# A two-model fp32 forward pass on one core: the first model's token mixing gets its first VectorE split earlier, its first gated scores on ScalarE, one product in a named PSUM bank, the rotary sines ahead of the splits; at two stage changes one split moves behind the normalisation

## The chip, the core and the metric

One core of one Trainium2 chip runs the whole program as one launch. The metric is the device time of that launch in microseconds (us). Runs of this kernel before the change took 2380.64 us (median of 3, from 2380.03 to 2381.09).

## What is computed

Two transformer models run one after the other, with float32 inputs and outputs. The change touches the first model only (two layers, width 1024, 256 tokens x and 256 context tokens z). Each of its layers is, in short:

```python
x, z = x + 0.5*g*ffn1(...), z + 0.5*g*ffn1(...)     # SwiGLU, hidden width 2816
px, pz = split_in(hx @ w_in), split_in(hz @ w_in)   # 15 kinds of columns
a = fourier_mix(p.fourier)                          # 2-D DFT
b = neighborhood_attention(na_q, na_k, na_v, ctx k and v, bias)
c = gla_output(bidir_gla(q, k, v, gates))           # gated linear attention, chunks
d = block_attention(rope(gqa_q), rope(gqa_k), gqa_v)
x = x + g*(concat(a, b, c, d) @ w_out)              # z as well, in layer 0 only
x = x + 0.5*g*ffn2(...)                             # z as well, in layer 0 only
```

Each sub-block starts with an RMS norm and a per-channel scale and shift (the modulation). The second model (two layers of softmax attention with forget gates beside retention, and a SwiGLU) follows on x and 16 meta tokens.

In the gated attention the score of query i and key j is a sum over 32 channels of q·k·decay. The kernel builds it by levels: a first, undecayed product q·k (times 2) gives the diagonal of each 128x128 tile, and seven masked levels overwrite the rest of it.

## The kernel before

**Weights and splits.** Every big product is done as three single-pass float32r matmuls: high weight times high input, high weight times low input, low weight times high input (lines 815 to 817). The weights stream from HBM in units of 128 x 1024 into a ring of six. For every unit ScalarE writes the high part into one of four `ring_high` buffers (line 1393) and VectorE writes the low part over the ring slot (line 1916), both in functions called `split_ahead`. ScalarE's split of a unit waits until TensorE has finished with the unit four splits earlier. TensorE's `weights()` waits for the low part. `split_ahead(1)` in step k of the mixing handles the unit that TensorE uses in step k + 4.

**The mixing.** A layer's `mixing` runs MIX_STEPS = 21 steps. TensorE, ScalarE and VectorE each have a function `mixing(l)` with the same step counter k; every engine works through its own list in order and the engines are tied by semaphores only. Step k does the projection of item k of PROJ1 (24 matmuls, about 5.8 us with 512 columns, half of it with 256) and, around it, small jobs. On TensorE the order within a step is: the attention scores of the tile whose turn is k + 1, the four products `gla_pairs(l, k - 10)` for 9 <= k <= 17, the projection, `head_mean`, the rope `rotation`, `turn` (transposes of the probabilities, line 1157), `values` (probabilities times V, line 1169). So step 9 does the first, undecayed pairs, number -1, and step 10 the pairs of level 0 (both line 1191). On VectorE step k does: the sines of rope items (`rope_sin`, line 2241), the row maxima of the scores (`maxima`, lines 2283 to 2308), the head norm (`qk_norm`, line 2229), the rope sum, `mixed_low` (line 2336: it reads what `values` left in its bank and so frees the bank), the doubling of the first pairs into `gla_scores` in step 9 (line 2421) or the masked copy of a level in steps 10 to 16 (line 2431), then `project`: the eviction of the projection (line 2211), `normalise` of the probabilities (line 2332), and the split of step k. On ScalarE step k does: `turned` (line 1647), `mixed_high` (line 1656), the squares for the head norm (line 1590), the decays' exponential (line 1713), the softmax exponentials (lines 1615 and 1616), its own evictions (line 1577), the high half of the split (line 1393), then the head norm's root (lines 1400 and 1403).

**PSUM banks.** TensorE has eight banks. `take(key)` gives the next one in rotation and first waits until what was in it, eight takes before, is freed; `take_at(b, key)` gives bank b by name, waits for its last user, and does not move the rotation. `gla_pairs` takes all its four banks before its first matmul.

```python
            def gla_pairs(l, v):
                ...
                ps = [take("pairs", l, v, h) for h in range(4)]
```

The takes around step 9 are, in order, in layer 0: scores (two, banks 7 and 0), pairs -1 (1, 2, 3, 4), projection 9 (5), a head mean (6), `values` of the z pair (7); then in step 10 scores (0, 1), pairs 0 (2, 3, 4, 5). In layer 1: scores (6, 7), pairs -1 (0, 1, 2, 3), projection 9 (4), a head mean (5), `values` (6); then in step 10, which has no scores, pairs 0 (7, 0, 1, 2).

**Stage changes.** When a sub-block's last product ends, its output chunks 0 to 7 (of 128 channels each) are added to the residual, squared, summed, and normalised for the next sub-block, for token group 0 (x) and then 1 (z). `norm(tag, g, chunks)` exists on VectorE (lines 1982 and 1991), ScalarE (lines 1441 and 1444) and GpSimd (line 636): VectorE scales a chunk, ScalarE adds the shift and rounds to the high part, and the low part comes from VectorE for even chunks and from GpSimd for odd ones. TensorE meanwhile begins the next sub-block's first units in `first_units`, chunk by chunk, group 0 and then group 1. `late_chunks` (ScalarE, line 1450 on) and `residual` (VectorE, line 2080 on) hold the order of these with the splits. The change's reordering is reached with group 1 after `out1` of layer 0 and after `ffn2` of layer 0, and leaves the order after `ffn1` as it was.

Of the kernel before, what the change touches and what calls it, by code (L numbers as in the profile page):

```python
# [32 lines left out]
ALU = mybir.AluOpType  # L33
# [3 lines left out]
P = 128  # L37
# [182 lines left out]
def build(nc, A, old=None):  # L220
    ev = Events(*(old or (None, None)))
    ctx = ExitStack()
    with ctx:
# [144 lines left out]
        def cst(at, n=P, rows=P):  # L368
            return const[0:rows, at:at + n]
# [412 lines left out]
        def _(pe):  # L782
# [378 lines left out]
            def values(pr):  # L1161
# [3 lines left out]
                p = take("attended", *pr["id"])  # L1165
# [96 lines left out]
            def mixing(l, prev):  # L1262
# [3 lines left out]
                for k in range(MIX_STEPS):  # L1266
# [19 lines left out]
                    for pr in owed_at(l, k):  # L1286
                        values(pr)
# [89 lines left out]
        def _(act):  # L1377
# [80 lines left out]
            def late_chunks(tag, h):  # L1458
# [19 lines left out]
                norm(tag, 1, range(4))  # L1478
                if tag[0] != "ffn1":
                    split_ahead(1)  # L1480
                norm(tag, 1, range(4, KC))
# [203 lines left out]
            def mixing(l):  # L1685
# [3 lines left out]
                for k in range(MIX_STEPS):  # L1689
# [20 lines left out]
                    if LEVEL_STEP - 1 <= k < LEVEL_STEP + LEVELS:  # L1710
# [67 lines left out]
            def second_mixing(l):  # L1778
                tp = ("b2", l)
                tiles = fox_tiles(l)  # L1780
                for k in range(FOX_STEPS):
# [18 lines left out]
                    if k == SLOT2[FLOG]:  # L1800
                        act.wait_ge(*when("forget_steps", "flog_neg_abs", l))
                        act.activation(negc[0:8, 1, :], negc[0:8, 1, :], ACT.Exp).then_inc(*made("flog_exp", l))
                        act.wait_ge(*when("flog_exp", l))
                        act.activation(negc[0:8, 1, :], negc[0:8, 1, :], ACT.Ln, bias=eps_one[0:8, 1:2]).then_inc(
                            *made("flog_ln", l))
# [4 lines left out]
                    if k == SLOT2[FLOG] + 1:  # L1810
                        act.wait_ge(*when("forget_steps", "negc", l))
                        act.wait_ge(*when("neg_cleared", l))
                        for e in range(2):
                            r = HD * e
                            act.activation(neg_parts[r:r + 8], negc[0:8, 2, :], ACT.Copy).then_inc(
                                *made("neg_high", l, e))
# [88 lines left out]
        def _(dve):  # L1905
# [175 lines left out]
            def residual(tag, l, m, streams, h, nb, last_part, dots_of=None):  # L2081
# [80 lines left out]
            def project(tag, plan, i, n, src, vtemp, tile=None, between=None, heads=(), items=()):  # L2162
                kind, dst, width = plan[i][:3]
                if i and plan[i - 1][0] == "V" and tag[0] == "mix1" and (i - 1) % 2 == 0:
# [10 lines left out]
                if not on_act(tag, i):  # L2175
# [21 lines left out]
                    elif kind == "T" and FOUR <= dst < FOUR + 2:  # L2197
# [3 lines left out]
                        dve.tensor_copy(x[:, :, P:SEQ], y[:, :, P:SEQ]).then_inc(*made("fold_steps", "upper", tag[1], dst - FOUR))  # L2201
                        dve.wait_ge(*when("fold_steps", "upper", tag[1], dst - FOUR))
                        dve.tensor_tensor(x[:, :, 1:P], y[:, :, 1:P], x[:, :, SEQ - 1:P:-1], ALU.add).then_inc(
                            *made("fold_steps", "even", tag[1], dst - FOUR))
                        dve.wait_ge(*when("fold_steps", "even", tag[1], dst - FOUR))
# [17 lines left out]
                if dst != FLOG:  # L2223
                    split_ahead(1)
# [167 lines left out]
            def mixing(l):  # L2392
# [4 lines left out]
                for k in range(MIX_STEPS):  # L2397
                    for i in means_at(l, k - 2):
                        if i >= 4:
                            rope_sin(tm, i - 4, cst(C_SIN1, NX), NX)  # L2400
# [16 lines left out]
                    if k == LEVEL_STEP:  # L2417
                        for h in range(4):
# [395 lines left out]
```

## Time and profile before

| | |
|---|---|
| runs before | 2380.64 us median (2380.03 to 2381.09) |
| the profiled execution's own time | 2380.5 us |
| its span, first to last instruction | 2378.7 us |
| TensorE matmuls busy | 2353.7 us (99%) |
| VectorE busy | 1533.4 us (64%) |
| ScalarE busy | 1014.2 us (43%) |
| GpSimd busy | 406.8 us (17%) |
| granted TensorE clock, mean | 0.999 |

PE is TensorE's matmul side and PEld its weight loads, DVE is VectorE, ACT ScalarE, POOL GpSimd. Layer 0's mixing lies at about 393 to 575 us of the span, layer 1's at about 1348 to 1485 us. A matmul's shown end is modelled and overlaps the next one's start, so where TensorE's time is summed the starts are compared. A timeline row gives the start, the time from the first start to the last end, the engine, the line, the operation, the tiles written and read, the shapes, the count of merged instructions, and in brackets the idle time before it with what ended that idle time.

### The profile page before, as it was taken

To read this page: it belongs to the slowest core of one execution; us is meant where nothing else is said; L and a number is where in the kernel's file an instruction comes from. 1 tells how busy PE (TensorE), PEld (TensorE's weight loads), DVE (VectorE), ACT (ScalarE), POOL (GpSimd) and SP (SyncE) were. 2 spreads that over 40 slices of the span, in tenths; PEclk is the share of its full clock that TensorE was granted. 3 is DMA by queue.
4 is the path that set the end of the run, shared out by engine and by line. 5 is a ranking of instruction groups with operands and counts; after the bars stand their busy time and mean duration, and the time that the engine had idled before them with its cause. 6 is when DMAs were issued, how large, how long until landed. Compare 5 with 4: busy or idle time off the path is not lost.

```text
span 2378.7 us, 36504 instructions
## 1 busy us (share of the span) xinstructions
PE 2353.7 (99%) x14394; PEld 2041.4 (86%) x14394; DVE 1533.4 (64%) x2611; ACT 1014.2 (43%) x1694; POOL 406.8 (17%) x427
## 2 busy tenths in 40 slices
PE   8999999999999999999999999999999999999998
PEld 6888889777888888888888877999889999989887
DVE  5888765884698865523323586766677665667874
ACT  5222224644522223422223465554455444456663
POOL 2221211240222131111011121121000220000110
PEclk9999999999999999999999999999999999999999
DMA  9565542112366654222222222555533555434553
GB/s 354 195 212 206 184 159 90 64 54 89 120 215 235 245 207 169 89 97 98 98 98 98 80 92 82 177 186 186 171 114 136 173 173 177 153 117 160 190 190 133
DMA packets 97865, 360.76 MB, mean 152 GB/s; under 512 B 11024, under 2 KB 11792, under 8 KB 96544
## 3 DMA queue, kind: packets, MB, share of 16 engines
q1 hardware_dynamic: 75744, 272.84, 33.2%
q0 software_dynamic: 21952, 85.59, 9.9%
q8 instruction: 115, 1.88, 0.3%
q14 instruction: 54, 0.44, 0.1%
HBM read 357.34 MB, written 1.05 MB: 151 GB/s over the span
## 4 chain that ended last, share of the span: by engine, by line
PE 94%; DVE 2%; ACT 1%; issue 1%; DMA 1%; POOL 0%; DVEq 0%; ACTq 0%; POOLq 0%
PE bank L815 26%; PE bank L817 25%; PE bank L816 25%; PE bank L822 6%; PE bank L823 3%; PE bank L1169 1%; PE bank L1139 1%; PE bank L1157 1%; PE bank L1191 1%; DVE ring_low L1916 1%; DMA arena<-w_mod_first_dram 1%; PE bank L1118 0%; PE bank L1078 0%; ACT ring_high L1393 0%; PE bank L1342 0%
## 5 line engine op out<-in xcount | busy, mean ns | idle before, releaser
L1916 DVE TENSOR_TENSOR ring_low<-ring,ring_high 128x1024 fp32r<-128x1024 f32 x520 | 642.0, 1235 | 484.3 <-ACT ring_high L1393 482.4
L815 PE MATMUL bank<-x_parts,ring_high 128*128 128x512 f32 (+2 forms) x2308 | 799.7, 347 | 4.8 <-POOL x_parts L636 2.2
L1393 ACT ACTIVATE ring_high<-ring 128x1024 fp32r<-128x1024 f32 x520 | 547.9, 1054 | 576.3 <-PE bank L817 532.9
L817 PE MATMUL bank<-x_parts,ring_low 128*128 128x512 f32 (+2 forms) x2308 | 786.2, 341 | 0.0
L816 PE MATMUL bank<-x_parts,ring_high 128*128 128x512 f32 (+2 forms) x2308 | 784.9, 340 | 0.0
L815 PEld LDWEIGHTS bank<-x_parts,ring_high 128*128 128x128 f32 x2308 | 434.5, 188 | 71.1 <-issue 13.3
L817 PEld LDWEIGHTS bank<-x_parts,ring_low 128*128 128x128 f32 x2308 | 434.6, 188 | 47.6
L816 PEld LDWEIGHTS bank<-x_parts,ring_high 128*128 128x128 f32 x2308 | 435.0, 188 | 47.0 <-issue 1.0
L646 POOL TENSOR_TENSOR hidden_parts<-fresh,hidden_parts 128x512 fp32r<-128x512 f32 (+2 forms) x132 | 204.1, 1547 | 1005.0 <-ACT hidden_parts L1527 1005.0
L1929 DVE CUSTOM_DVE_ANT_0 mod_products<-mod_ring,csilu 128x1024 bf16<-128x1024 f32 x224 | 300.5, 1378 | 31.8 <-DMA mod_ring<-w_mod_dram 30.5
L815 PE MATMUL bank<-hidden_parts,ring_high 128*128 128x512 f32 (+2 forms) x814 | 280.9, 345 | 0.7 <-POOL hidden_parts L646 0.7
L817 PE MATMUL bank<-hidden_parts,ring_low 128*128 128x512 f32 (+2 forms) x814 | 280.1, 344 | 0.0
L816 PE MATMUL bank<-hidden_parts,ring_high 128*128 128x512 f32 (+2 forms) x814 | 280.1, 344 | 0.0
L815 PEld LDWEIGHTS bank<-hidden_parts,ring_high 128*128 128x128 f32 x814 | 153.6, 189 | 19.3 <-POOL hidden_parts L646 1.1
L816 PEld LDWEIGHTS bank<-hidden_parts,ring_high 128*128 128x128 f32 x814 | 153.6, 189 | 18.2
L817 PEld LDWEIGHTS bank<-hidden_parts,ring_low 128*128 128x128 f32 x814 | 153.5, 189 | 18.0
L1516 ACT ACTIVATE act_out<-bank 128x512 f32<-128x512 f32 x66 | 39.6, 600 | 263.6 <-PE bank L817 263.6
L822 PE MATMUL bank<-x_parts,ring_high 128*128 128x512 f32 x352 | 123.2, 393 | 0.0
L822 PE MATMUL bank<-hidden_parts,ring_high 128*128 128x512 f32 x308 | 106.9, 392 | 0.0
L815 PE MATMUL bank<-early_parts,ring_high 128*128 128x258 f32 x352 | 99.9, 284 | 0.0
L817 PE MATMUL bank<-early_parts,ring_low 128*128 128x258 f32 x352 | 99.3, 282 | 0.0
L816 PE MATMUL bank<-early_parts,ring_high 128*128 128x258 f32 x352 | 99.3, 282 | 0.0
(267 smaller groups left out, 2757.7 us busy)
## 6 DMA issues: line engine op xcount, KB each, us to landing
ring<-stream_dram SPq DMA_DIRECT2D x517, 512.0 KB, 3.3
mod_ring<-w_mod_dram POOLq DMA_DIRECT2D x128, 512.0 KB, 4.4
arena<-w_mod_first_dram POOLq DMA_DIRECT2D x8, 1024.0 KB, 11.8
ring<-stream_dram POOLq DMA_DIRECT2D x3, 512.0 KB, 10.6
arena<-na_bias_dram POOLq DMA_DIRECT2D x2, 768.0 KB, 12.1
mod_ring<-consts_dram POOLq DMA_DIRECT2D x1, 1076.0 KB, 5.3
resid<-x_dram POOLq DMA_DIRECT2D x2, 512.0 KB, 5.9
resid<-ctx_dram POOLq DMA_DIRECT2D x2, 512.0 KB, 7.1
```

What stands on the lines that cost most here:

```text
L646: pool.tensor_tensor(lo[:, f], fresh[:, f % 2, 0:n], hi[:, f].bitcast(F32), ALU.subtract).then_inc(*made("hidden_low", tag, h, f))
L815: pe.matmul(out, w[0][:, b], xh, start=start, stop=False)
L816: pe.matmul(out, w[0][:, b], xl, start=False, stop=False)
L817: return pe.matmul(out, w[1][:, b], xh, start=False, stop=stop)
L822: pe.matmul(bank.rearrange("p (k n) -> p k n", k=2), w[0][:, b], both, start=start, stop=False)
L823: return pe.matmul(bank[:, 0:NX], w[1][:, b], high, start=False, stop=stop)
L1139: mm = pe.matmul(out, pr["q"][r, q:q + nq], pr["k"][r, 0:NZ if twin else nk], start=not fox, stop=True, skip_group_check=nq < P)
L1157: mm = pe.transpose(p[0:rows, kt * P:kt * P + nq], probs[0:nq, b, e, kt * P:kt * P + rows], cst(C_IDENT, nq, nq))
L1393: act.activation(high[:, i % SPLIT], ring[:, u % LOADED], ACT.Copy).then_inc(high_parts, 1)
L1516: act.activation(act_out[:, f % 2, 0:n], p[:, 0:n], ACT.Silu).then_inc(*made("silu", tag, h, f, frees=("gate", tag, h, f)))
L1916: dve.tensor_tensor(low[:, u % LOADED], ring[:, u % LOADED], high_f[:, i % SPLIT], ALU.subtract).then_inc(low_parts, 1)
L1929: dve.tensor_tensor_reduce(junk[:, s], mod_ring[:, n % MOD_RING], csilu[:, s], 1.0, 0.0, ALU.mult, ALU.add, mod[:, l, s, j:j + 1]).then_in ...
```

## The change

It does six things; the renamed semaphore families (`fold_steps` and `first_sum_steps` become `gate_steps`, `flog_exp`, `flog_ln` and `neg_high` become `forget_act`) are increments and waits of the same instructions under another name.

```diff
 PE:   def values(pr, b=None):
                 pe.wait_ge(*when(*pr["v_ready"]))
                 for j in range(len(pr["tiles"])):
                     pe.wait_ge(*when("probs_t", *pr["id"], j))
-                p = take("attended", *pr["id"])
+                p = take("attended", *pr["id"]) if b is None else take_at(b, "attended", *pr["id"])
...
                     for pr in owed_at(l, k):
-                        values(pr)
+                        values(pr, ev.banks["pairs", l, -1, 0] if k == LEVEL_STEP else None)
...
 ACT:  late_chunks
                 root_of_mean(tag, 1)
-                norm(tag, 1, range(4))
+                norm(tag, 1, range(KC))
                 if tag[0] != "ffn1":
                     split_ahead(1)
-                norm(tag, 1, range(4, KC))
...
 ACT:  mixing, after the decays' exponential, before exps
+                    if k == LEVEL_STEP:
+                        for h in range(4):
+                            act.wait_ge(*when("pairs", l, -1, h))
+                            p = bank("pairs", l, -1, h)
+                            act.activation(gla_s[:, h, 0:n // P], p[:, 0:n].rearrange("p (t n) -> p t n", n=P), ACT.Copy,
+                                           scale=2.0).then_inc(*made("gla_first", l, h, frees=("pairs", l, -1, h)))
...
 DVE:  residual
-                norm(tag, 1, range(4))
+                norm(tag, 1, range(KC))
                 if tag[0] != "ffn1":
                     split_ahead(1)
-                norm(tag, 1, range(4, KC))
...
 DVE:  project
+                if i == 0 and tag[0] == "mix1":
+                    split_ahead(1)
...
                 for item in items:
                     qk_norm(tag[1], item)
-                if dst != FLOG:
+                for item in rotated:
+                    rope_sin(tag, item - 4, cst(C_SIN1, NX), NX)
+                if dst != FLOG and (i or tag[0] != "mix1"):
                     split_ahead(1)
...
 DVE:  mixing
-                    for i in means_at(l, k - 2):
-                        if i >= 4:
-                            rope_sin(tm, i - 4, cst(C_SIN1, NX), NX)
...
-                    if k == LEVEL_STEP:
-                        for h in range(4):
-                            dve.wait_ge(*when("pairs", l, -1, h))
-                            p = bank("pairs", l, -1, h)
-                            dve.tensor_scalar(gla_s[:, h, 0:ntile], p[:, 0:n].rearrange("p (t n) -> p t n", n=P), 2.0,
-                                              None, ALU.mult).then_inc(
-                                                  *made("gla_scores", l, -1, h, frees=("pairs", l, -1, h)))
...
-                            dve.wait_ge(*when("gla_scores", l, v - 1, h))
+                            dve.wait_ge(*(when("gla_scores", l, v - 1, h) if v else when("gla_first", l, h)))
...
                         project(tm, PROJ1, k, width1(l, PROJ1[k]), proj1, VTEMP1, turns.get(k + 1),
-                                items=root_first(l, k))
+                                items=root_first(l, k), rotated=[i for i in means_at(l, k - 1) if i >= 4])
```

In words: (1) `values` of step 9 goes into the bank of the first pairs' head 0 instead of the next in rotation. (2) The doubling of the first pairs goes from VectorE to ScalarE. (3) In step 0 VectorE does its split before it waits for the projection. (4) The rope sines are done at the end of the step before, ahead of that step's split, not after it. (5) and (6) After `out1` and `ffn2` of layer 0 the fourth split comes behind all eight chunks of group 1's norm, on ScalarE and on VectorE.

## Rows read from the trace of the kernel before

**Rows 1.** The page: the chain that ended last, by engine.
```profile
PE 94%; DVE 2%; ACT 1%; issue 1%; DMA 1%; POOL 0%; DVEq 0%; ACTq 0%; POOLq 0%
```

**Rows 2.** Waits of TensorE, 1344 to 1480 us (layer 1's mixing): total, times, longest.
```profile
PE bank L1169 <- ACT arena L1616: 1.6, 1, 1.6
PE bank L815 <- DVE ring_low L1916: 1.6, 1, 1.6
PE bank L1191 <- DVE arena L2211: 1.1, 1, 1.1
```

**Rows 3.** Timeline of the stage change after `out1` of layer 0, several engines.
```profile
629.81 1.23 DVE L1916 TENSOR_TENSOR ring_low<-ring,ring_high 128x1024 fp32r<-128x1024 f32 x1 [1.05 <-ACT ring_high L1393]
...
632.55 0.39 PE L815 MATMUL bank<-x_parts,ring_high 128*128 128x256 f32 x1
...
633.93 0.38 PE L815 MATMUL bank<-x_parts,ring_high 128*128 128x256 f32 x1 [0.40 <-POOL x_parts L636]
...
639.06 0.40 PE L815 MATMUL bank<-x_parts,ring_high 128*128 128x512 f32 x1
```

**Rows 4.** The same after `ffn2` of layer 0.
```profile
994.99 1.23 DVE L1916 TENSOR_TENSOR ring_low<-ring,ring_high 128x1024 fp32r<-128x1024 f32 x1 [1.05 <-ACT ring_high L1393]
...
999.11 0.38 PE L815 MATMUL bank<-x_parts,ring_high 128*128 128x256 f32 x1 [0.40 <-POOL x_parts L636]
```

**Rows 5.** Timeline, layer 1, steps 0 to 4: ScalarE, VectorE, TensorE.
```profile
1362.02 1.04 ACT L1393 ACTIVATE ring_high<-ring 128x1024 fp32r<-128x1024 f32 x1
...
1365.42 1.06 ACT L1393 ACTIVATE ring_high<-ring 128x1024 fp32r<-128x1024 f32 x1 [2.09 <-PE bank L817]
...
1371.26 0.69 ACT L1400 ACTIVATE rstd<-bank,eps_one 128x512 f32<-128x512 f32 x1 [0.32 <-PE bank L1118]
...
1365.42 0.69 DVE L2211 TENSOR_SCALAR arena<-bank 128x512 f32<-128x512 f32 x1 [3.38 <-PE bank L817]
1366.03 2.35 DVE L1916 TENSOR_TENSOR ring_low<-ring,ring_high 128x1024 fp32r<-128x1024 f32 x2
...
1367.30 0.50 PE L815 MATMUL bank<-x_parts,ring_high 128*128 128x512 f32 x1 [1.56 <-DVE ring_low L1916]
```

**Rows 6.** Timeline, layer 1, steps 8 to 10: TensorE.
```profile
1405.54 1.02 PE L1118 MATMUL bank<-squares,const 128*128 128x512 f32 x2
1408.15 1.95 PE L1169 MATMUL bank<-arena 128*64 128x256 f32 x16 [1.58 <-ACT arena L1616]
1410.03 0.73 PE L1191 MATMUL bank<-mod_ring 32*128 32x128 f32 x16
```

**Rows 7.** The same steps: VectorE, then ScalarE.
```profile
1412.11 0.42 DVE L2336 TENSOR_TENSOR mixed_parts<-bank,mixed_parts 128x256 fp32r<-128x256 f32 x1
...
1406.95 0.51 ACT L1615 ACTIVATE arena<-arena,softmax_stats 128x256 f32<-128x256 f32 x1 [3.70 <-DVE softmax_stats L2302]
...
1411.32 0.37 ACT L1656 ACTIVATE mixed_parts<-bank 128x256 fp32r<-128x256 f32 x1
```

**Rows 8.** Timeline, layer 0, steps 9 and 10: TensorE, VectorE, ScalarE.
```profile
465.83 1.17 PE L1191 MATMUL bank<-mod_ring 32*128 32x128 f32 x32
...
468.39 0.41 DVE L2336 TENSOR_TENSOR mixed_parts<-bank,mixed_parts 128x256 fp32r<-128x256 f32 x1
...
463.00 0.60 ACT L1577 ACTIVATE arena<-bank 128x512 f32<-128x512 f32 x1 [2.84 <-PE bank L817]
```

**Rows 9.** Timeline, layer 0, step 11: VectorE, TensorE.
```profile
476.34 0.42 DVE L2241 TENSOR_TENSOR fresh<-bank,const 128x256 f32<-128x256 f32 x1
...
477.01 1.17 PE L1191 MATMUL bank<-mod_ring 32*128 32x128 f32 x32 [0.66 <-DVE fresh L2241]
```

**Rows 10.** Stretches: us, busy of PE, PEld, DVE, ACT, POOL, granted clock, DMA share, GB/s.
```profile
2369.00:2373.80 4.80, 0.94 (x5) 0.34 (x3) 2.63 (x7) 1.31 (x3) 0.00 (x0) 1.00 0.00 0
2373.80:2378.70 4.90, 0.00 (x0) 0.00 (x0) 1.81 (x5) 0.00 (x0) 0.00 (x0) 0.50 0.52 214
1405.70:1408.20 2.50, 0.92 (x5) 0.12 (x4) 2.50 (x12) 1.25 (x5) 1.18 (x4) 1.00 0.51 184
```

More of the change, by code:

```diff
@@ L1159, in turn, with values @@
                     mm.then_inc(*made("turned", *pr["id"], j, e))
-            def values(pr):
+            def values(pr, b=None):
                 pe.wait_ge(*when(*pr["v_ready"]))
@@ L1801, in second_mixing @@
                         act.wait_ge(*when("forget_steps", "flog_neg_abs", l))
-                        act.activation(negc[0:8, 1, :], negc[0:8, 1, :], ACT.Exp).then_inc(*made("flog_exp", l))
-                        act.wait_ge(*when("flog_exp", l))
+                        act.activation(negc[0:8, 1, :], negc[0:8, 1, :], ACT.Exp).then_inc(*made("forget_act", "exp", l))
+                        act.wait_ge(*when("forget_act", "exp", l))
                         act.activation(negc[0:8, 1, :], negc[0:8, 1, :], ACT.Ln, bias=eps_one[0:8, 1:2]).then_inc(
-                            *made("flog_ln", l))
+                            *made("forget_act", "ln", l))
                     if k in tiles:
@@ L2200, in project @@
                         dve.tensor_copy(x[:, :, 0:1], y[:, :, 0:1])
-                        dve.tensor_copy(x[:, :, P:SEQ], y[:, :, P:SEQ]).then_inc(*made("fold_steps", "upper", tag[1], dst - FOUR))
-                        dve.wait_ge(*when("fold_steps", "upper", tag[1], dst - FOUR))
+                        dve.tensor_copy(x[:, :, P:SEQ], y[:, :, P:SEQ]).then_inc(*made("gate_steps", "upper", tag[1], dst - FOUR))
+                        dve.wait_ge(*when("gate_steps", "upper", tag[1], dst - FOUR))
                         dve.tensor_tensor(x[:, :, 1:P], y[:, :, 1:P], x[:, :, SEQ - 1:P:-1], ALU.add).then_inc(
-                            *made("fold_steps", "even", tag[1], dst - FOUR))
-                        dve.wait_ge(*when("fold_steps", "even", tag[1], dst - FOUR))
+                            *made("gate_steps", "even", tag[1], dst - FOUR))
+                        dve.wait_ge(*when("gate_steps", "even", tag[1], dst - FOUR))
                         dve.tensor_tensor(x[:, :, P + 1:SEQ], y[:, :, P - 1:0:-1], x[:, :, P + 1:SEQ],
@@ L2533, in forget_gates @@
                 if k == SLOT2[FLOG] + 1:
-                    dve.wait_ge(*when("flog_ln", l))
+                    dve.wait_ge(*when("forget_act", "ln", l))
                     dve.scalar_tensor_tensor(e, y, 0.0, e, ALU.min, ALU.subtract).then_inc(*made("forget_steps", "flog_log", l))
@@ L2543, in forget_rest @@
                 dve.wait_ge(*when("forget_steps", "negc", l))
-                dve.wait_ge(*when("neg_high", l, 1))
+                dve.wait_ge(*when("forget_act", "neg_high", l, 1))
                 for e in range(2):
@@ L2621, in _ @@
                 dve.tensor_tensor(scaled[:, 0:4, a:b], scaled[:, 0:4, a:b], scaled[:, 4:8, a:b], ALU.add).then_inc(
-                    *made("first_sum_steps", "first_fours", g))
-                dve.wait_ge(*when("first_sum_steps", "first_fours", g))
+                    *made("gate_steps", "first_fours", g))
+                dve.wait_ge(*when("gate_steps", "first_fours", g))
                 dve.tensor_tensor(scaled[:, 0:2, a:b], scaled[:, 0:2, a:b], scaled[:, 2:4, a:b], ALU.add).then_inc(
-                    *made("first_sum_steps", "first_twos", g))
-                dve.wait_ge(*when("first_sum_steps", "first_twos", g))
+                    *made("gate_steps", "first_twos", g))
+                dve.wait_ge(*when("gate_steps", "first_twos", g))
                 dve.tensor_tensor(sumsq[:, a:b], scaled[:, 0, a:b], scaled[:, 1, a:b], ALU.add).then_inc(
```

4 lines of the change are left out of this document (2 added, 2 removed).

## The prediction

> **What bounds the kernel now.** I read the page's busy times and its chain by engine first, then TensorE's waits, then the timelines around each of those waits. TensorE is 94% of the chain [rows 1], and the change removes no matmul. So it can only give or take TensorE's idle gaps, and only those in the first model's two mixings and at two stage changes. In layer 1's mixing the waits come to 1.6, 1.6 and 1.1 us plus smaller ones [rows 2], in layer 0's to one of 0.7 us that matters [rows 9], and each stage change has one near 0.4 us [rows 3, 4]. All of it together is near 6 us of 2380, and 0.2% of the time is 4.8 us, about what a measurement of this kernel can tell from no change. I look at starts, since a matmul's shown end overlaps the next start.
>
> **Fourth split last.** After `out1` of layer 0 VectorE idles 1.05 us for ScalarE's high half and then splits for 1.14 us (629.81 to the next instruction at 630.95) before it normalises chunks 4 to 7 of group 1 [rows 3]. TensorE starts chunk 4 at 632.55 and chunk 5, for which it waited on GpSimd, at 633.93; the six matmuls between take 0.82 when nothing waits (0.12 from start to start, and 0.1 more for the first after a stop), so 0.56 us are lost, and before 632.55 another 0.19 us. With the split behind, the chunks come 1.05 + 1.14 = 2.2 us earlier, more than both losses: minus 0.75 us. The moved split then ends near 634.2 instead of 631.0; TensorE starts that unit at 639.06 now [rows 3], 638.3 then, so the split has 4 us of cover, and without it every us beyond would be paid. After `ffn2` of layer 0 the rows are the same to 0.01 us [rows 4] (0.56 and 0.17 lost): minus 0.73. Sum **minus 1.5 us**. No DMA is issued by the moved steps; ScalarE's table load behind the norm comes 1.1 us sooner.
>
> **Step 0's split first.** In layer 1 TensorE could start step 4 at 1365.58 and starts at 1367.30, when the first low half is written (the merged row at 1366.03 holds the splits of steps 0 and 1) [rows 5]. Its high half was ready at 1363.06, while VectorE idled 3.38 us for the projection. Done then, it ends near 1364.2, and the 1.72 us go. What is late next: VectorE's split of step 1 has to wait for its own high half, 1366.48 [rows 5], so the gate's eviction comes 0.65 to 0.7 us sooner, and ScalarE, which then does the gate's shift, a high half and the roots back to back, starts the first root 1.09 us sooner than 1371.26 (it loses its 0.32 us of idle as well) [rows 5]. From there to step 9 the chain runs through VectorE and ScalarE, not TensorE, so the waits in steps 6 and 9 (0.5 and 1.1 us) keep their place in that chain and TensorE reaches the first pairs **1.09 us earlier**, not 1.72. In layer 0 TensorE has no wait there, so I take nothing.
>
> **First pairs on ScalarE.** VectorE loses four instructions in each layer. ScalarE gains four. No row has this copy on ScalarE; the nearest is its eviction of 128x512 at 0.60 us each [rows 8], so at most 2.4 us in layer 0, and half at 256 columns. It stands before the softmax exponentials, behind which ScalarE idles 2.84 us in layer 0 [rows 8] and in front of which it idles 3.70 us in layer 1 [rows 7]. That is the cover: cost nothing. If it were gone, the exponentials and the evictions queued behind them would be late by up to 2.4 us. The gain on VectorE is nothing either: in layer 1 it waits for those exponentials and then for the next high half.
>
> **Values in the pairs' bank.** Here two waits trade places. Now, in layer 1, `values` takes the bank of the scores in rotation, and waits for the exponentials (L1616) until 1408.15; the means before it began at 1405.54 and need 0.86, so 1.75 us are lost [rows 6]. In the new bank it needs only the first of ScalarE's four copies, long done. That wait goes. But the next four takes are the pairs of level 0, and since the rotation was not moved, they reach the bank that `values` has just filled: in layer 1 they take banks 6, 7, 0, 1 in the old numbering and `values` sits in 0; in layer 0, 1, 2, 3, 4 and `values` sits in 1. All four are taken before the first matmul, so step 10's pairs and the projection behind them wait for `mixed_low` (L2336) of that very pair, on VectorE in step 10.
> - Layer 0: TensorE starts these pairs at 465.83, and L2336 ends at 468.80 [rows 8], because VectorE first does the maxima of scores that TensorE ends just before the pairs, and a head norm. New start 468.84: **plus 3.0 us**.
> - Layer 1: L2336 runs 1412.11 to 1412.53, behind ScalarE's roots and `mixed_high` [rows 7]; 1.09 us earlier that is 1411.44, a start at 1411.48 against 1410.03 now [rows 6]: **plus 1.45 us**, with the 1.09 and the 1.75 already in it. TensorE then stands idle for about 4.2 us in one piece.
>
> Behind both, VectorE and ScalarE have been waiting for TensorE's projection, so the delay passes whole to the end. The later bank waits keep their distance of eight takes.
>
> **The clock in that gap.** The longest stop of TensorE in the steady part is the one before 1408.15, and the granted clock there is 1.00; after the last matmul (1.00 up to 2373.80) it is 0.50, that is 1.2 instead of 2.4 GHz [rows 10]. By these rows a gap of 4.2 us lies between what did not cost the clock and what did. The Trainium skill ("TensorE: Matmul & The Clock Gate", "HAM oscillation — how this bites in real kernels") says that a gap in TensorE's work can bring the slow clock back, so that the next matmuls start cold. By rows 10 alone the sum stays as it is; by that rule the rival below is due.
>
> **Sines ahead of splits.** In layer 0 the pairs of level 1 wait for the bank of the rotation, freed by L2241 after a split of 1.14 us: start 477.01 where 476.28 was possible [rows 9]. With the sine ahead the wait goes: minus 0.7 us. The splits come 0.4 us later and are used four steps on. In layer 1 nothing waits there. The remaining fold wait (0.4 us) is not touched.
>
> **Sum.** Against the profiled execution's own 2380.5 us (its span 2378.7): minus 1.5; layer 0 plus 3.0 minus 0.7; layer 1 plus 1.45. That is plus 2.3, 2382.8 us; the median of the runs is 0.1 above that execution, so **2382.9 us**. Ends of the unknowns: the first layer's pairs between plus 2.5 and plus 3.5; ScalarE's copies 0 to plus 1.2; the 1.09 between 0.5 and 1.72 (1 us either way). With these alone, 2380.8 to 2385.2.
>
> **Rivals.**
> - *The clock falls in the new gap.* Against it: rows 10's third row. For it: the second. Price: no row shows a matmul at 1.2 GHz; a projection of 5.8 us would take twice that, so between 0 and plus 5.8; I take half, plus 2.9: 2385.8 us. It decides if the gap in layer 1 is above 4 us. Chance 0.18.
> - *The bank is free in time* (the other side, faster). If `mixed_low` were through when the pairs ask, before 465.83 in layer 0 and 1407.3 in layer 1, the change would give all it removes: 1.5 + 0.7 + 1.09 + 1.75 = 5.0 us, 2375.6 us. For it: only that VectorE is relieved of L2421. Against it: L2336 waits for scores and roots, not for VectorE's time. Chance 0.12.
> - *Nothing arrives.* The gains are taken back by the VectorE and ScalarE chain, and the new bank wait is half of mine: 2380.6 us. For it: the chain of steps 4 to 9 already eats a third of the first gain. Chance 0.09.
> - The forecast: 0.61.
>
> **Numbers.** Faster than 2375.9: three quarters of the second rival, 0.09. Slower than 2385.4: two thirds of the first and 0.07 of the forecast's tail, 0.19. Within: 0.72. The range takes the forecast's own ends, the clock rival with half of its upper price, and stops short of the fast rival: 2377.0 to 2387.5.
>
> **What would show it.** Right: TensorE's waits list L1191 behind DVE L2336 twice, near 3.0 and 4.2 us; the waits behind ACT L1616, DVE L1916 (1.6 us) and DVE L2241 are gone; the third wait at the stage changes (POOL L636) shrinks by 0.8 us over both. Wrong: if level 0's pairs start without a wait in step 10, the bank step fails and the time is near 2375.6; if the granted clock shows 0.50 anywhere between 1408 and 1425 us, the first rival holds; if step 4 of layer 1 still waits for L1916, the first split is not early.

## The result, and the profile after

| | before | after |
|---|---|---|
| median of 10 runs on the same chip | 2380.44 us (2379.88 to 2381.09) | 2386.78 us (2384.26 to 2388.50) |
| ratio | | 1.0027, 95% interval 1.0019 to 1.0035 |
| the profiled execution's own time | 2380.5 us | 2384.26 us, the fastest of the ten |
| its span | 2378.7 us | 2382.5 us |
| mean granted clock over the ten runs | 0.999 | 0.996 to 0.999 |

The change makes the kernel slower by 6.3 us, 0.27%. Two things are in this table besides the loss: the runs spread over 4.2 us where those of before spread over 1.2, and the profiled execution, whose rows follow, is 2.5 us below the median. So the rows can explain 3.8 us, and 2.5 us need runs.

TensorE's waits over the whole span, the rows that concern the change (line, releaser: us in total, times, longest). The small ones answer to [rows 2] and to the brackets in [rows 3, 4, 9].

```profile
PE bank L1191 <- DVE mixed_parts L2344: 4.3, 1, 4.3
PE bank L1191 <- issue: 2.9, 1, 2.9
...
PE bank L815 <- POOL x_parts L636: 1.4, 4, 0.4
...
PE bank L1191 <- DVE arena L2217: 1.1, 1, 1.1
...
PE bank L1191 <- DVE gla_scores L2429: 0.3, 1, 0.3
PE bank L815 <- POOL hidden_parts L646: 0.2, 1, 0.2
```

Gone are the waits behind the exponentials (1.6 us), behind the first low half (1.6) and behind the sine (0.7); the wait at the two stage changes fell from 2.2 us in all to 1.4. In their place stand 4.3 and 2.9 us ahead of the first level's pairs (L1191).

Layer 0, steps 9 and 10, VectorE and TensorE (answers to [rows 8]):

```profile
467.66 0.74 DVE L2237 SCALAR_TENSOR_TENSOR arena<-arena,small,rstd 128x512 f32<-128x512 f32 x1
468.32 0.42 DVE L2344 TENSOR_TENSOR mixed_parts<-bank,mixed_parts 128x256 fp32r<-128x256 f32 x1
468.83 1.17 PE L1191 MATMUL bank<-mod_ring 32*128 32x128 f32 x32 [2.91 <-issue]
```

"issue" is what the profile writes when it sees no releaser; the pairs start 0.09 us after L2344 ends, and one run below moves that instruction alone.

Layer 1, the same place, with ScalarE (answers to [rows 6, 7]):

```profile
1405.61 1.95 PE L1169 MATMUL bank<-arena 128*64 128x256 f32 x16
...
1410.42 0.36 ACT L1655 ACTIVATE mixed_parts<-bank 128x256 fp32r<-128x256 f32 x1
...
1410.55 0.75 DVE L2237 SCALAR_TENSOR_TENSOR arena<-arena,small,rstd 128x512 f32<-128x512 f32 x1
...
1411.22 0.42 DVE L2344 TENSOR_TENSOR mixed_parts<-bank,mixed_parts 128x256 fp32r<-128x256 f32 x1
...
1411.89 0.73 PE L1191 MATMUL bank<-mod_ring 32*128 32x128 f32 x16 [4.34 <-DVE mixed_parts L2344]
```

`values` (L1169) no longer waits for the exponentials. It is done at 1407.55, and then TensorE stands still for 4.34 us.

Stretches of the same execution (us, busy of PE, PEld, DVE, ACT, POOL, granted clock, DMA share, GB/s):

```profile
470.00:474.30 4.30, 4.30 (x21) 3.56 (x20) 2.59 (x4) 1.54 (x4) 2.96 (x5) 1.00 0.01 4
...
1407.60:1411.80 4.20, 0.00 (x0) 0.00 (x0) 3.56 (x7) 3.98 (x10) 0.11 (x1) 1.00 0.00 1
...
1412.80:1416.20 3.40, 3.40 (x9) 2.65 (x9) 1.30 (x4) 0.00 (x0) 1.64 (x5) 0.50 0.00 0
1416.20:1420.00 3.80, 3.80 (x18) 3.13 (x18) 0.08 (x1) 0.08 (x1) 0.00 (x0) 1.00 0.00 0
```

Here is the term that the forecast left out. The clock held through the gap of layer 1 and for 0.9 us of work after it, then stood at 0.50 for 3.4 us, at 1.2 GHz in place of 2.4, and came back. In those 3.4 us TensorE was busy without a stop and got through 9 matmuls; in the next 3.8 us it did 18. Behind layer 0's gap of 2.9 us the clock held, in this execution.

Starts of the same TensorE instruction in both traces, compared all along the span, give the whole account of this execution. The offset is the start after the change less the start before it. It stays level for long stretches, and a step is the difference between the level behind a place and the level ahead of it:

| place (time in the trace before) | step, us | offset behind it | forecast |
|---|---|---|---|
| pairs of level 0, layer 0 (465.83; offset ahead of it +0.03) | +2.98 | +3.01 | +3.0 |
| pairs of level 1, layer 0 (477.01) | -0.73 | +2.28 | -0.7 |
| rest of layer 0's mixing (480 to 500) | -0.08 | +2.20 | none |
| first sum of squares at the end of `out1` (610.3) | +0.28 | +2.48 | none |
| stage change after `out1` (632.55 to 634.3) | -0.94 | +1.54 | -0.75 |
| hidden parts of layer 0's `ffn` (750.07) | -0.42 | +1.12 | none |
| stage change after `ffn2` (997.73 to 999.5) | -0.92 | +0.20 | -0.73 |
| step 4 of layer 1 (1367.30) | -1.87 | -1.67 | -1.72 |
| steps 6 to 8 (1382.70, 1387.04) | +0.49, +0.29 | -0.89 | together +0.63 |
| `values` of layer 1 (1408.15) | -1.66 | -2.55 | -1.75 |
| pairs of level 0, layer 1 (1410.03) | +4.42 | +1.87 | +4.29 |
| half clock behind it | +1.57 | +3.44 | 0 |
| pairs of level 1, layer 1 (1424.27) | +0.34 | +3.78 | none |
| sum | | last start +3.79 | +2.3 |

### The profile page after: what moved, and what is told of

Read it like the earlier page. It is cut to its first block and busy times, and to the rows that moved or that the text cites. A ratio compares the mean times of both kernels' runs of the same rounds, so it can differ in the third digit from the quotient of the medians.

```text
span 2382.5 us, 36500 instructions
## 1 busy us (share of the span) xinstructions
PE 2355.2 (99%) x14394; PEld 2042.8 (86%) x14394; DVE 1533.1 (64%) x2603; ACT 1016.6 (43%) x1702; POOL 404.6 (17%) x427
## 5 line engine op out<-in xcount | busy, mean ns | idle before, releaser
L646 POOL TENSOR_TENSOR hidden_parts<-fresh,hidden_parts 128x512 fp32r<-128x512 f32 (+2 forms) x132 | 203.3, 1540 | 1005.4 <-ACT hidden_parts L1526 1005.4
```

The lines of the kernel that those rows point to most:

```text
L646: pool.tensor_tensor(lo[:, f], fresh[:, f % 2, 0:n], hi[:, f].bitcast(F32), ALU.subtract).then_inc(*made("hidden_low", tag, h, f))
```

## The experiments

Twelve kernels, each timed in five rounds beside the kernel before on the same chip. The medians of before in the three sets were 2380.68 us (first four kernels), 2380.63 (next four) and 2380.19 (last four); each difference from before below is against its own. Where kernels of different sets are compared with each other, or with the changed kernel (its own before: 2380.44), the medians are taken as they stand, and some 0.4 us of such a difference can be the set. The 95% interval of a ratio reaches about 0.0009, or 2 us, to either side, so that of a single part of the change (kernels 7 to 9) the starts in the trace tell more than the median. A line number moves by a few lines between the kernels.

### 1. Without the named bank

```diff
-                        values(pr, ev.banks["pairs", l, -1, 0] if k == LEVEL_STEP else None)
+                        values(pr)
```

(on the changed kernel)

> The changed kernel with the values taking the next bank of the rotation again; everything else of the change stays. Theory (the named bank is the whole loss: 3.0 us in layer 0, 2.5 us in layer 1, and about 1.7 us of half clock behind layer 1's gap): the other parts are all that is left, 0.9 + 0.6 us at the two stage changes, 0.7 us of the sine wait, 0.9 to 1.1 us at layer 1's steps 4 to 10, so about 2380.4 - 3.2 = 2377.2 us, granted clock 1.00 from end to end of both mixing stages. Rival (the other parts are worth nothing by themselves, or one of them pulls the clock down): 2380 to 2382 us. Rival (the bank is not the cause): 2386.8 us as the changed kernel.

Measured: 2377.74 us (2377.06 to 2378.25), ratio 0.9988 (0.9979 to 0.9997), 2.9 us below the kernel before and 9.0 below the changed one. Layer 1 there, TensorE:

```profile
1404.55 1.95 PE L1169 MATMUL bank<-arena 128*64 128x256 f32 x16 [1.59 <-ACT arena L1615]
1406.42 0.73 PE L1191 MATMUL bank<-mod_ring 32*128 32x128 f32 x16
```

The pair of waits is back as in [rows 6]: 1.59 us behind the exponentials, none ahead of the pairs, and the granted clock is 1.00. The bank is the whole loss; everything else of the change, taken together, gains.

### 2. The named bank alone

```diff
-            def values(pr):
+            def values(pr, b=None):
...
-                p = take("attended", *pr["id"])
+                p = take("attended", *pr["id"]) if b is None else take_at(b, "attended", *pr["id"])
...
-                        values(pr)
+                        values(pr, ev.banks["pairs", l, -1, 0] if k == LEVEL_STEP else None)
```

(on the kernel before)

> The kernel before with the named bank alone. Theory: TensorE's first pair starts 3.0 us later in layer 0; in layer 1 at the end of VectorE's mixed_low (12.53 us in place of 10.03, so 2.5 us later), and behind that gap the granted clock falls to 0.50 for some 3.4 us, which costs 1.7 us more. Sum 2380.4 + 3.0 + 2.5 + 1.7 = 2387.7 us. Rival (the clock does not fall, since the gap here is cut by the wait for the exps that the kernel before has): 2386.0 us. Rival (the gap's loss is recovered at the next wait of TensorE for a bank or an operand, as layer 0 showed nothing of step 0's gain): 2383 us or less.

Measured: 2390.22 us (2388.31 to 2390.97), plus 9.5 us, 2.5 more than expected. TensorE in layer 0 and in layer 1:

```profile
469.09 1.17 PE L1191 MATMUL bank<-mod_ring 32*128 32x128 f32 x32 [2.91 <-issue]
...
470.82 0.63 PE L817 MATMUL bank<-x_parts,ring_low 128*128 128x512 f32 x1
471.25 0.63 PE L815 MATMUL bank<-x_parts,ring_high 128*128 128x512 f32 x1
...
1411.85 1.95 PE L1169 MATMUL bank<-arena 128*64 128x256 f32 x16 [1.03 <-DVE gla_scores L2421]
1417.04 1.24 PE L1191 MATMUL bank<-mod_ring 32*128 32x128 f32 x16 [3.25 <-DVE mixed_parts L2336]
```

and its stretches:

```profile
470.80:474.10 3.30, 3.30 (x9) 2.60 (x8) 2.08 (x4) 1.08 (x2) 2.18 (x4) 0.50 0.00 0
...
1416.50:1423.00 6.50, 5.96 (x27) 4.77 (x28) 1.72 (x5) 0.26 (x1) 2.76 (x5) 0.50 0.00 1
```

Three things. The same gap of 2.91 us that left the clock alone in the changed kernel's profile made it fall here: a 128x512 matmul starts every 0.43 us in place of 0.23, and TensorE's offset to before grows from 3.26 to 4.84 us; 0.2 of these 1.6 us come back at the next wait (477.01). So layer 0's gap can cost 1.4 us more. In layer 1 the clock was already at 0.50 while TensorE still waited, and the work after it lost 2.7 us (offset 7.01 to 9.75). And `values` now waits 1.03 us for VectorE's first gated scores, which free its bank (L2421). That costs nothing more, since the gap behind it is as much shorter (3.25 in place of 4.3 us): from `values` to the pairs the steps are -0.54 and +3.31, together +2.77, where the changed kernel has -1.66 and +4.42, +2.76. The 2.5 us beyond my 2387.7 are nearly all clock: 1.4 in layer 0, for which I had put nothing, and 2.7 in place of 1.7 in layer 1.

### 3. The gap filled, too long

```diff
+                    for _ in range(FILL[l]):
+                        pe.matmul(ps[at][:, 0:NX], cst(C_ONES64), cst(C_COS1, NX), start=True, stop=True)
```

(on the changed kernel, ahead of the level-0 pairs; `FILL = (10, 16)`)

> The changed kernel with TensorE kept busy in the gap ahead of the first level's pairs: 10 products of constants in layer 0, 16 in layer 1, each 64 rows x 256 columns of fp32 into a pairs bank that is already free and that the first pair clears. The pairs start no earlier. Theory (the waits cost 2.2 us net, the half clock behind layer 1's gap the other 1.7 us, and the few tenths of half clock in some runs more make the spread of 2384.3 to 2388.5): granted clock 1.00 through both mixing stages, 2384.3 - 1.7 = 2382.6 us, with runs within 0.5 us of each other. Rival (the clock is not what costs the 4 us that the forecast lacked): 2386.8 us as the changed kernel, or more by what the filling products overrun the gap.

Measured: 2389.27 us (2388.28 to 2389.97). TensorE:

```profile
465.92 4.58 PE L1198 MATMUL bank<-const 128*128 128x256 f32 x20
...
1410.74 7.14 PE L1198 MATMUL bank<-const 128*128 128x256 f32 x32 [0.76 <-ACT arena L1635]
1417.82 0.73 PE L1211 MATMUL bank<-mod_ring 32*128 32x128 f32 x16
```

A product shows as two records of 0.229 us, twice the length I had reckoned with, and the fill began behind a bank wait. It ran past the gap in both layers, by 1.6 us in layer 0 and by 3.7 in layer 1 (pairs at 1417.82, L2364 done at 1414.07). The time says nothing of the clock; but with the clock at 1.00 throughout, the runs lie within 1.7 us of each other.

### 4. The fourth split last, alone

```diff
-                norm(tag, 1, range(4))
+                norm(tag, 1, range(KC))
                 if tag[0] != "ffn1":
                     split_ahead(1)
-                norm(tag, 1, range(4, KC))
```

(on the kernel before, VectorE and ScalarE)

> The kernel before with the fourth split behind the norms at the stage changes, alone. Theory (each of the two changes of stage gains what the changed kernel's trace shows of it, 0.65 us after the first output projection and 0.28 + 0.56 us after the feed-forward): 2380.4 - 1.5 = 2378.9 us. Rival (part of it was only the reading of one execution, or the later fourth split makes the next projection wait): 2379.7 to 2380.4 us.

Measured: 2378.32 us (2378.01 to 2379.20), minus 2.4 us, ratio 0.9991 (0.9982 to 1.0000). By starts: -0.93 and -0.92 at the two stage changes, together 1.85, and -0.53 at the hidden parts of layer 0's `ffn`, a place that the edit does not touch (see the last section).

### 5. The gap filled to size

```diff
+                    pe.wait_ge(*when("free", *waits[3]))
+                    for _ in range(FILL[l]):
+                        pe.matmul(ps[3][:, 0:NX], cst(C_ONES64), cst(C_COS1, NX), start=True, stop=True)
+                    for u in waits[0:3]:
+                        pe.wait_ge(*when("free", *u))
```

(on the changed kernel; `FILL = (5, 9)`)

> Again the changed kernel with TensorE kept busy ahead of the first level's pairs, now sized by what the first filling showed (0.229 us for each of the two records of a 256-column fp32 product, so 0.458 us a product) and started as soon as the last of the four banks is free, long before the values' bank: 5 products (2.3 us) in layer 0, 9 (4.1 us) in layer 1, inside gaps of 2.9 and 4.3 us. Theory (after layer 1's gap the clock falls and costs 1.7 us, in layer 0 in some runs another 1.2 us, which makes the changed kernel's spread of 2384.3 to 2388.5): granted clock 1.00 through both mixing stages, the pairs start where they did, 2386.8 - 2 to 3.5 = 2383.0 us give or take 0.7, and runs within 1.2 us of each other. Rival (the clock costs nothing that the waits do not): 2386.8 us.

Measured: 2383.18 us (2382.62 to 2384.33), mean clock 0.999 in all 11 runs. TensorE, then its stretches:

```profile
466.09 2.43 PE L1194 MATMUL bank<-const 128*128 128x256 f32 x10
469.02 1.17 PE L1207 MATMUL bank<-mod_ring 32*128 32x128 f32 x32 [0.51 <-DVE mixed_parts L2360]
...
1408.07 4.15 PE L1194 MATMUL bank<-const 128*128 128x256 f32 x18
1412.38 0.73 PE L1207 MATMUL bank<-mod_ring 32*128 32x128 f32 x16 [0.16 <-DVE mixed_parts L2360]
```

```profile
1405.60:1411.90 6.30, 6.30 (x36) 4.38 (x34) 4.82 (x15) 5.21 (x15) 0.99 (x3) 1.00 0.24 83
1411.90:1418.00 6.10, 5.94 (x40) 4.64 (x39) 1.78 (x6) 0.31 (x1) 2.77 (x5) 1.00 0.00 0
```

The pairs start where they did (steps of +2.9 and +4.3 us, in the changed kernel +3.0 and +4.4), nothing useful was added, and 3.6 us are gone from the median (3.8 if each kernel is taken against its own before). That is the clock's share of the loss. In layer 0 the row now names L2360, the low parts, as the releaser that "issue" hid.

### 6. A bank that nothing asks for

```diff
-                        values(pr, ev.banks["pairs", l, -1, 0] if k == LEVEL_STEP else None)
+                        values(pr, ev.banks["pairs", l, -1, 3] if l and k == LEVEL_STEP else None)
```

(on the changed kernel)

> The changed kernel with the values' bank named only in layer 1, and there the bank of the last of the four first pairs, which nothing takes again until after the projection; in layer 0 the rotation. Theory: without a bank that the level-0 pairs need, all that is lost is gone as in the kernel with the rotation (2377.7 us), and the wait for the exps in layer 1 (1.58 us before the change) goes as well: 2377.7 - 1.2 to 1.75 = 2376.0 to 2376.5 us. Rival (another wait stands right behind the exps, such as the head mean's or the pairs' operands): 2377.7 us.

Measured: 2376.26 us (2376.01 to 2377.13), ratio 0.9982 (0.9973 to 0.9991), faster than before by 4.4 us and than the changed kernel by 10.5. TensorE in layer 1:

```profile
1403.36 1.95 PE L1169 MATMUL bank<-arena 128*64 128x256 f32 x16
1406.10 0.73 PE L1191 MATMUL bank<-mod_ring 32*128 32x128 f32 x16 [0.79 <-ACT arena L1615]
```

`values` waits for nothing, but the pairs take the banks of the scores next and wait 0.79 us for the same exponentials. By starts half of the 1.6 us comes in (-0.82 against kernel 1 in layer 1), and the other half is the next wait. The theory had the whole of it, and the median, 1.5 us below kernel 1's, is where the theory put it. The rows do not show the other 0.7 us: outside that place the two traces differ by 0.2 us from the start and in one step, at the hidden parts of the last section, a wait that moves from run to run. So the hit on the number is in part luck.

### 7. Step 0's split first, alone

```diff
+                if i == 0 and tag[0] == "mix1":
+                    split_ahead(1)
...
-                if dst != FLOG:
+                if dst != FLOG and (i or tag[0] != "mix1"):
                     split_ahead(1)
```

(on the kernel before, VectorE)

> The kernel before with step 0's split ahead of the step's other VectorE work, alone. By the changed kernel's trace: step 4 of layer 1 starts 1.8 us earlier, and 0.3 + 0.3 us of it is lost again at the norms of the first operands and about 0.4 at the pairs' operand: 2380.6 - 0.8 to 1.1 = 2379.5 to 2379.8 us. Rival (the wait for the exps ahead of the level-0 pairs, or another release that hangs on no split, takes all of it): 2380.6 us.

Measured: 2379.11 us (2378.71 to 2380.06), minus 1.5 us, ratio 0.9995 (0.9986 to 1.0004). VectorE, layer 1:

```profile
1362.42 1.23 DVE L1916 TENSOR_TENSOR ring_low<-ring,ring_high 128x1024 fp32r<-128x1024 f32 x1 [1.05 <-ACT ring_high L1393]
1364.70 0.69 DVE L2213 TENSOR_SCALAR arena<-bank 128x512 f32<-128x512 f32 x1 [1.06 <-PE bank L817]
```

The split now stands in the idle time ahead of the projection [rows 5]. By starts: -1.87 at step 4, then +0.49 and +0.29, which leaves -1.09 at the pairs, the same three steps as in the changed kernel; -0.44 more is again at layer 0's hidden parts. No step is seen in layer 0's mixing.

### 8. The first gated scores on ScalarE, alone

```diff
-                            dve.tensor_scalar(gla_s[:, h, 0:ntile], p[:, 0:n].rearrange("p (t n) -> p t n", n=P), 2.0,
-                                              None, ALU.mult).then_inc(
-                                                  *made("gla_scores", l, -1, h, frees=("pairs", l, -1, h)))
...
+                            act.activation(gla_s[:, h, 0:n // P], p[:, 0:n].rearrange("p (t n) -> p t n", n=P), ACT.Copy,
+                                           scale=2.0).then_inc(*made("gla_first", l, h, frees=("pairs", l, -1, h)))
```

(on the kernel before)

> The kernel before with the four first gated scores taken by ScalarE (one activation each in place of VectorE's tensor_scalar), alone. Forecast: nothing waits for them, 2380.6 us within 0.3. Rival (VectorE's 1.08 us for three of them, which stand ahead of the softmax in layer 1, is on the path to the exps and the values' bank): 2379.5 to 2380.0 us. Rival (ScalarE's copies push its exps or decays back by 1 to 1.5 us): 2381.5 us or more.

Measured: 2380.46 us (2379.88 to 2380.98), 0.2 us below before, ratio 1.0000 (0.9991 to 1.0009): nothing. By starts neither layer's mixing has a step from it.

### 9. The sines ahead, alone

```diff
-                    for i in means_at(l, k - 2):
-                        if i >= 4:
-                            rope_sin(tm, i - 4, cst(C_SIN1, NX), NX)
...
+                for item in rotated:
+                    rope_sin(tag, item - 4, cst(C_SIN1, NX), NX)
                 if dst != FLOG:
```

(on the kernel before)

> The kernel before with the rotations' sines ahead of the step's split, alone. Theory (from the kernels so far: TensorE's wait for a bank behind the sine in layer 0, 0.66 us, goes, and in layer 1 a wait of 0.37 us for the level-0 scores comes, which stands in every kernel that has the sines ahead and in none that has not): 2380.6 - 0.6 + 0.4 = 2380.4 us. Rival (the 0.37 us is not the sines' doing): 2380.0 us. Rival (nothing, the sine's wait is replaced by another): 2380.6 us.

Measured: 2379.48 us (2379.07 to 2380.37), minus 0.7 us, ratio 0.9996 (0.9987 to 1.0005). By starts -0.73 at 477.01 and no step in layer 1. My theory that layer 1's new 0.37 us come from the sines fell; the gain is the forecast's.

### 10. The free bank, sines in layer 0 alone

```diff
-                                items=root_first(l, k), rotated=[i for i in means_at(l, k - 1) if i >= 4])
+                                items=root_first(l, k), rotated=[i for i in means_at(l, k - 1) if i >= 4 and l == 0])
```

(on kernel 6, with layer 1's sines put back to where the kernel before has them)

> The kernel with the free bank in layer 1 (e6_free_bank_layer1, 2376.3 us) with the sines ahead in layer 0 alone. Theory (layer 1's sines cost 0.37 us at the level-0 scores): 2375.9 us. Rival (they don't): 2376.3 us, and TensorE's wait for the level-0 scores of layer 1 still reads 0.4 us.

Measured: 2376.27 us (2375.95 to 2377.10). The median is that of kernel 6, though 3.9 us below its own before where kernel 6 is 4.4 below; the starts in the two traces stay within 0.2 us of each other, and the row is still there:

```profile
PE bank L1191 <- DVE gla_scores L2433: 0.4, 1, 0.4
```

So that wait is not the sines'. It stands in every kernel that combines the changes and in none that has one of them alone (2, 4, 7, 8, 9); which of them together make it was not tried. The same holds of the +0.28 us at 610.3 in the table above.

### 11. Layer 1's gap alone filled

```diff
-FILL = (5, 9)
+FILL = (0, 9)
```

(on kernel 5)

> The changed kernel with TensorE kept busy in layer 1's gap alone (9 products), layer 0's gap left idle. Theory (layer 1's half clock costs 1.7 us in every run, layer 0's 1.2 to 1.5 us in most runs and nothing in the profiled one): median 2383.2 + 1.2 to 1.5 = 2384.5 us, with single runs at 2383 where layer 0's clock holds; in a run where it falls the rows show 0.50 behind the first pairs of layer 0. Rival (all of the clock's cost is layer 1's): 2383.2 us as with both gaps filled.

Measured: 2384.50 us (2383.06 to 2386.41). The mean clock is 0.999 in the two fastest runs (2383.06 and 2383.61, the profiled one) and 0.998 in the nine others. In the profiled execution layer 0's gap is there and the clock did not fall:

```profile
PE bank L1207 <- issue: 3.0, 1, 3.0
```

```profile
470.00:474.30 4.30, 4.30 (x25) 3.51 (x20) 2.59 (x4) 1.42 (x3) 2.85 (x5) 1.00 0.01 4
```

So of the clock's 3.6 us the median holds 2.3 in layer 1 (2386.78 less 2384.50) and 1.3 in layer 0 (2384.50 less 2383.18). With each kernel against its own before it is 2.0 and 1.8, so the sum is better known than its parts. That the fall behind layer 0's 2.9 us comes and goes from run to run, and the spread with it, is read from the mean clocks (0.999 in all runs of kernel 5, 0.998 in nine of eleven here) and from kernel 2's row.

### 12. Layer 0's low parts first

```diff
+                    first = l == 0 and k == LEVEL_STEP + 1
+                    if first:
+                        for pr in owed_at(l, k - 1):
+                            mixed_low(pr)
                     if k + 1 in turns:
                         maxima(*turns[k + 1])
```

(on the changed kernel, VectorE; the later call is left out there)

> The changed kernel with VectorE taking the low parts of the values (which free the named bank) ahead of the softmax's maxima and the head norm in layer 0's step 10; nothing else. Theory (layer 0's 3.0 us are VectorE's order: 2.3 us of other work stand ahead of the 0.4 us that frees the bank): the gap shrinks to 0.5 to 0.9 us, no half clock behind it, 2386.8 - 2.3 - 1.2 to 1.5 = 2383.1 us give or take 0.5. Rival (the softmax of step 10, 0.4 us later, makes TensorE wait elsewhere for as long): 2383.5 us or more. Rival (the bank is free late for another reason): 2386.8 us.

Measured: 2383.11 us (2382.33 to 2384.22), 3.7 below the changed kernel. VectorE and TensorE in layer 0, and TensorE in layer 1:

```profile
466.16 0.42 DVE L2344 TENSOR_TENSOR mixed_parts<-bank,mixed_parts 128x256 fp32r<-128x256 f32 x1 [0.28 <-ACT mixed_parts L1655]
...
466.69 1.17 PE L1191 MATMUL bank<-mod_ring 32*128 32x128 f32 x32 [0.71 <-issue]
...
1409.55 1.24 PE L1191 MATMUL bank<-mod_ring 32*128 32x128 f32 x16 [4.33 <-DVE mixed_parts L2344]
```

```profile
1406.00:1407.00 1.00, 0.00 (x0) 0.00 (x0) 0.63 (x3) 1.00 (x2) 0.00 (x0) 1.00 0.00 0
...
1407.50:1408.00 0.50, 0.00 (x0) 0.00 (x0) 0.50 (x1) 0.47 (x2) 0.00 (x0) 0.50 0.00 0
```

One instruction moved on VectorE takes 2.2 of layer 0's 3.0 us away (the step at the pairs is +0.79 in place of +2.98), which shows that this wait was VectorE's order, and behind a gap of 0.7 us the clock holds. The other 1.5 us of the median fit the half clock of layer 0, which goes with the long gap. In layer 1 nothing was changed: the gap is 4.33 us as before, the clock fell inside it this time, and the half-rate work after it lost 2.1 us.

## Why the prediction was right or wrong

The forecast was 2382.9 us, the median is 2386.8: inside the range, near its upper end, and slower by more than 0.2%, to which the prediction gave 0.19. The likeliest case did not come. The first rival did, at 2386.8 in place of its 2385.8. The range held because it had kept room for that rival, not because the sum was right.

**The bank.** This step held to 0.2 us. Layer 0: plus 3.0 forecast, plus 2.98. Layer 1 up to the pairs, with the split and the exponentials in it: plus 1.45 forecast; -1.87 + 0.49 + 0.29 - 1.66 + 4.42 = plus 1.67. It could be foreseen because all four pairs' banks are taken ahead of the first matmul, and the rotation runs into the bank just filled. Kernels 1, 2 and 12 show it from three sides.

**The splits, the sines, the copies.** Fourth split: -1.5 forecast, -1.86 in the changed kernel, -1.85 alone. The forecast left in the 0.1 us that the first matmul after a stop takes more; where the stop goes this goes too, two times at each stage change. First split: forecast -1.72 at step 4, of which -1.09 arrive; measured -1.87 and -1.09, in the changed kernel and alone. Sines: -0.7; -0.73 in the changed kernel and alone. Copies on ScalarE: 0, alone -0.2, within the noise; with the named bank they are worth nothing either (kernel 2's +2.77 against +2.76).

**The step that failed** is "The clock in that gap": "By rows 10 alone the sum stays as it is", and with it the rival's chance of 0.18. The rows read were a gap of about 1.6 us at clock 1.00 and the end of the kernel at 0.50. A gap of 4.2 us lies between them, and I took the near one as if it bounded the far one; there was no row that excluded the fall. The measured cost: 3.6 us of the median (kernel 5), nearly the whole miss of 3.9. With the clock kept up the kernel takes 2383.2 us, 0.3 from the forecast. The trace before also held the price of half rate, which the prediction did not use: at the start of the span the products of line 913 (128x256) start every 0.43 us up to 4.8 us and every 0.21 us after 5.1, although the clock column prints 1.00 for both.

**The rival was right in kind and wrong in two sizes.** Its price, 2.9 us for layer 1, was half of a projection at half rate; the row shows 3.4 us at half rate and 1.6 lost, the medians 2.0 to 2.3. And its condition, "if the gap in layer 1 is above 4 us", looked at one gap only: layer 0's gap of 2.9 us, for which I had reserved nothing, costs 1.3 to 1.8 in the median and 1.4 in kernel 2. The Trainium skill ("TensorE: Matmul & The Clock Gate", "HAM oscillation — how this bites in real kernels") puts the penalty at half of the throttled time. The traces come a little below that, at 0.46 of the work done at 0.50: 1.57 of 3.4 us behind layer 1's gap here, 1.58 of 3.4 in kernel 2's layer 0, and in kernel 2's layer 1, where TensorE still waited for the first 0.9 us of the stretch, 2.7 of 5.95.

**Small terms not forecast.** +0.34 us at the level-0 scores of layer 1 and +0.28 at 610.3, open as said; and -0.42 at layer 0's hidden parts.

**Two slips in the sums.** The lower end of the forecast alone, 2380.8 us, does not follow from its terms: 2382.9 less 0.5 and less 0.6 to 1.0 is 2381.4 to 2381.8. And "Nothing arrives" was priced at the time before, which leaves nothing for the half of the bank wait that it keeps (at least 1.5 us in layer 0). Neither changed the range.

**"Nothing arrives" and "the bank is free in time"** are both out: each gain arrived to 0.1 us or came out larger, and L1191 waited in both layers. But what the second one priced is nearly what kernel 6 gives: 2376.3 us against the 2375.6 that all gains without the bank's loss would make.

## What to carry to other kernels

Naming a buffer by hand takes its holder out of the rotation but leaves the rotation's next takers where they were: list who takes that buffer next and when its reader is through, before counting the wait that goes. A TensorE gap is to be priced twice, as its length and as the work after it at half rate; where no row of the trace shows a gap of that length, the slow outcome belongs in the forecast with a price and a chance of its own, and a spread of the runs that widens with a change is a sign of it. Idle products sized to the gap tell the two prices apart in one run.

## What the runs showed of the hardware that was not expected

**The fall of the clock is not a matter of the gap's length alone.** The same gap of about 2.9 us in layer 0 left the clock at 1.00 in the profiled executions of the changed kernel and of kernel 11, and brought 0.50 from about 470.7 us on in kernel 2. Layer 1's gap of 4.3 us was followed by the fall at 1412.8 us, 0.9 us after work had resumed, in the changed kernel, and had the fall inside it, at about 1407.3 us, in kernel 12. A stretch at 0.50 lasted 3.4 us in the first case and near 7 in the last, and the work lost 1.6 and 2.1 us. In kernel 2's layer 1 a gap of 3.25 us had the fall inside it as well, at about 1416.2 us. What decides between them was not tested.

**A wait far from the change moves by up to 1.2 us.** TensorE's wait for GpSimd's `hidden_parts` (L646) near 750 us reads 0.7 us before, 0.2 in the changed kernel, none in kernels 1, 4 and 12, 1.0 to 1.2 in kernels 3, 9, 10 and 11, and 0.2 to 0.8 in the others:

```profile
PE bank L815 <- POOL hidden_parts L646: 1.1, 1, 1.1
```

(kernel 9, whose profiled execution took 2380.37 us against a median of 2379.48; kernel 10's, with 1.0 us, 2377.10 against 2376.27.) Ahead of that work VectorE waits for a chunk of modulation weights from DMA, so its place shifts with the arrival; that this is the cause is read from the rows and was not tried. It is the size of the spread within most of these kernels, and it makes a difference of half a microsecond between two profiles worth nothing unless the starts are compared place by place.
